# On VectorE, the second set of masks of the scan ahead of the turn of the next tile's raw blocks

## The chip, the cores and the metric

The kernel runs on one core of one Trainium2 chip. The metric is the device time of one execution in microseconds, lower is better. Five engines work side by side, each on its own queue of instructions: TensorE (PE, matrix products and transposes), VectorE (DVE), ScalarE (ACT), GpSimd (POOL) and SyncE (SP), which here only issues transfers. They meet at semaphores that the program names itself.

## The reference

One inference step of a one-layer backbone over 17 tiles of 128 tokens: 16 tiles of latent tokens and one of context. Only the time-mixing part matters here, a recurrence in two directions with 8 heads and a 64 x 64 state:

```python
def step(S, inp):
    r_t, w_t, k_t, v_t, kk_t, kka_t = inp
    sa = jnp.einsum('bdhvk,bdhk->bdhv', S, kk_t)
    S = (S * w_t[..., None, :] - sa[..., :, None] * kka_t[..., None, :]
         + v_t[..., :, None] * k_t[..., None, :])
    return S, jnp.einsum('bdhvk,bdhk->bdhv', S, r_t)

s_final, ys = lax.scan(step, s0.astype(f32), xs)
```

Before it the tokens are normed, modulated and projected; after it three branches are gated, merged and projected, and a mixture of 16 experts and a final norm follow.

## The kernel before

The stages run one after the other: tokens (`stage_tokens`), the recurrence (`stage_scan`), the merge, the routing, the experts, and the last norm. `stage_scan` takes most of the time between 950 and 1900 us of the profiled span, and only it is touched.

**How the scan works.** It walks over 17 tiles, in both directions at once (`d` is the direction, `g` one of two groups of four heads). Within a tile the recurrence is written in block form, so that it turns into products of 128-token blocks and the inverse of a triangular 128 x 128 matrix for each head. Products of scaled rows give four sets of blocks: the raw blocks `Ar` (Q by B), from which the inverse is made, and the mixed blocks `ArbT`, `AqkT` and `ArkT`. VectorE multiplies each mixed set by a triangular mask on its way out of PSUM: four instructions for each set (two directions by two groups), at line L1253. These are the masks in the title.

**The inverse goes round through DRAM, a tile ahead.** In step `q` the raw blocks of tile `q + 1` are made (TensorE `raw`, copied out by ScalarE at L1063). Those of direction 1 must be turned first: `turn_raw` on VectorE (two transposes into `AT`, tile name b_at, semaphore `at_ok`). ScalarE then writes their diagonal blocks to DRAM (`backward_out`, L927), as SyncE does for direction 0 (`forward_out`). When all eight small writes have landed (`a_st`), SyncE reads them back in another layout (`diagonal_in`, b_ta, L947), GpSimd inverts them (`invert`, L918 and L921), SyncE writes the result out (`inverse_out`, s_t, L955) and, in the step after, places it in `TZ` (`inverse_in`, b_tz, L967), which VectorE turns and TensorE uses.

**SyncE's queue is in order.** In one step it issues: `inverse_out(q)`, `forward_out(q + 1)`, `inverse_in(q)`, `diagonal_in(q + 1)`, then the four loads of the input rows of tile `q + 2` (`front`, in `load_front`, L133; semaphore `f_in[d]`, 2.5 MB), then the outputs of the last tile and the next values. All that stands behind `diagonal_in` waits with it.

**Who waits for the input rows.** On ScalarE `own_decay(q + 2, d)` (an exponential, L1029) waits for `f_in[d]` and stands ahead of the copies `u6` (L1131) and `tl` (L1135) that TensorE's product `w6` of the present tile needs. On TensorE `cumulate(q + 2, d)` (two products of 128 x 512 for each direction in the records) waits for `f_in[d]` and stands right ahead of `w6`. Both exist in steps 0 to 14.

**TensorE's order in a step** is: transposes, raw products of tile `q + 1`, the mixed products (`arb`, `aqk`, `ark`), then XX (state and `AqkT` by values, reads `aqk_ok`), the inverse's steps u5, w5, u6, the transposes `tl`, `cumulate`, w6, the product u, the new state n, and the outputs y. The masks of `AqkT` are what XX waits for. The last step (tile 16) has no next tile, so no `turn_raw` and no `cumulate`.

`over_tiles` writes steps 0, 1, 14, 15 and 16 out and runs steps 2 to 13 in a loop of two steps each. The order of every engine is that of the program text; nothing is scheduled behind it.

Of the kernel before, what the change touches and what calls it, by code (L numbers as in the profile page):

```python
# [87 lines left out]
def after(e, sem, t, per=1):  # L88

    e.wait_ge(sem, t * per + per)  # L90


def freed(e, sem, t, per=1):

    if not (isinstance(t, int) and t == 0):
        e.wait_ge(sem, t * per)
# [702 lines left out]
def stage_scan(nc, io, scr, K):  # L799
# [3 lines left out]
    with ExitStack() as ctx:  # L803
# [3 lines left out]
        def each(name, shape):  # L807
            return [sb(f"b_{name}{d}", shape) for d in range(2)]
# [15 lines left out]
        def by_four(ap):  # L824
            return ap.rearrange("p (j n) -> p j n", j=4)
# [14 lines left out]
        ArbT, AqkT, ArkT = (each(n, [P, H, P]) for n in ("arbT", "aqkT", "arkT"))  # L840
# [52 lines left out]
        def heads(g):  # L893
            return slice(4 * g, 4 * g + 4)

        def over_group(c):
            return const[:, c, :].unsqueeze(1).broadcast_to([P, 4, P])

        def flat(ap):
            return ap.rearrange("p a n -> p (a n)")  # L900

        def bank(d, i):
            return ps[:, 4 * d + i, :]

        def by_head(ap):
            return ap.rearrange("p (h n) -> p h n", h=H)
# [22 lines left out]
        with nc.Block() as block:  # L929
# [249 lines left out]
            def _(dve):  # L1179
# [3 lines left out]
                def turn(out, src, g):  # L1183

                    return v_.transpose(flat(out[:, heads(g), :]), flat(src[:, heads(g), :]))

                def before_token(t, d):

                    after(dve, f_in[d], t, 32)
                    after(dve, x_ok[d], t)  # L1190
                    v_.tensor_tensor(EX[d][:, :], F[d][:, FKK, :], EX[d][:, :], ALU.mult).then_inc(kx_ok[d], 1)

                def scaled_q(t, d):
                    after(dve, e_ok[d], t)
                    after(dve, kx_ok[d], t)
                    freed(dve, qT_ps[d], t)
                    v_.tensor_tensor(Qt[d][:, :], EX[d][:, :], EI[d][:, :], ALU.mult).then_inc(q_ok[d], 1)

                def scaled_b(t, b, d):

                    if not (isinstance(t, int) and t < 2):
                        after(dve, n_ps[d], t - 2)
                    after(dve, e_ok[d], t)
                    v_.scalar_tensor_tensor(Bt[d][b][:, :], F[d][:, FKA, :], -1.0, EN[d][:, :], ALU.mult, ALU.mult)\
                        .then_inc(b_ok[d], 1)

                def turn_raw(t, b):
                    freed(dve, a_st, t, 128)
                    for d, g in (PAIRS[0][1], PAIRS[1][0]):
                        after(dve, ar_ok[1][g], t)  # L1210
                        turn(AT, Ar[1][b], g).then_inc(at_ok, 1)

                def scaled_state(own, d, factor):
                    return v_.tensor_tensor(Shd[d][own, :, own], SN[d][own, :, :],
                                            factor[own].broadcast_to([64, 4, N]), ALU.mult)
# [21 lines left out]
                def step(q, b, n, left):  # L1237
                    if left > 1:
                        for d in range(2):
                            after(dve, pm_ok[d], q + 1)  # L1240
                            after(dve, shd_ok[d], q)
                            v_.tensor_tensor(fac[d][:, :].unsqueeze(2), PM[d][b][:, :, 1:2], PM[d][1 - b][:, :, 0:1], ALU.mult)\
                                .then_inc(fac_ok[d], 1)
                    for d in range(2):
                        after(dve, rT_ps[d], q)
                        v_.tensor_copy(flat(RT[d][:, :, :]), bank(d, 0)).then_inc(rT_ok[d], 1)
                    for out, p_ps, p_ok, at, masks in ((ArbT, arb_ps, arb_ok, (0, 2), (UPI, LOWI)),
                                                       (AqkT, aqk_ps, aqk_ok, (1, 3), (UP, LOW)),
                                                       (ArkT, ark_ps, ark_ok, (0, 2), (UPI, LOWI))):
                        for r, pair in enumerate(PAIRS):  # L1250
                            for d, g in pair:
                                after(dve, p_ps[d][g], q)
                                v_.tensor_tensor(out[d][:, heads(g), :], by_four(bank(d, at[r])), over_group(masks[d]), ALU.mult)\  # L1253
                                    .then_inc(p_ok[d][g], 1)
                        if out is ArbT and left > 0:
                            turn_raw(q + 1, 1 - b)
                    for d in range(2):
                        after(dve, tz_in[d], q, 64)
                        for g in range(2):
                            turn((TIT[0], TI[1])[d], TZ[d], g).then_inc(turn_ok[d][g], 1)  # L1260
                    for d, g in GROUPS:
                        after(dve, w5_ps[d][g], q)
                        after(dve, turn_ok[d][g], q)
                        v_.tensor_tensor(TIT[d][:, heads(g), :], (TIT[0], TZ[1])[d][:, heads(g), :],
                                         by_four(bank(d, 2 * g + 1)), ALU.add).then_inc(tr5_ok[d][g], 1)
                    if left > 1:
                        for d in range(2):
                            before_token(q + 2, d)
                    for d in range(2):
                        after(dve, w6_ps[d], q)  # L1270
                        v_.tensor_copy(TIT[d][LO[d], :, HI[d]], by_head(bank(d, 1))[LO[d]]).then_inc(t6_ok[d], 1)
                    if left > 1:
                        for d in range(2):
                            scaled_q(q + 2, d)
                    for d in range(2):

                        after(dve, n_ps[d], q)
                        after(dve, shd_ok[d], q)
                        new = by_four(bank(d, 2))
                        for u in range(2):  # L1280
                            own = slice(64 * u, 64 * u + 64)
                            ins = v_.tensor_tensor(SN[d][own, :, :], Shd[d][own, :, own], new[own, :, own], ALU.add)
                        ins.then_inc(sn_ok[d], 1)
                    if left > 1:
                        for d in range(2):
                            scaled_b(q + 2, b, d)
                    for d in range(2):
                        after(dve, y_ps[d], q)
                        freed(dve, y_st[d], q, 16)
                        v_.tensor_copy(Yo[d][:, :], bank(d, 1)).then_inc(y_ok[d], 1)  # L1290
                        after(dve, sn_ok[d], q)
                        if left > 1:
                            after(dve, fac_ok[d], q)
                            for u in range(2):
                                ins = scaled_state(slice(64 * u, 64 * u + 64), d, fac[d][:, :].unsqueeze(2))
                            ins.then_inc(shd_ok[d], 1)
                        elif left == 1:
                            v_.memset(Shd[d][:, :, :], 0.0).then_inc(shd_ok[d], 1)
                        else:
                            v_.tensor_tensor(SN[d][:, :, :], SN[d][:, :, :], PM[d][b][:, :, 1:2].broadcast_to([P, 4, N]),  # L1300
                                             ALU.mult).then_inc(s_ok[d], 1)

                over_tiles(dve, step)

            @block.tensor
# [1202 lines left out]
```

## Time and profile before

| | us |
|---|---|
| median of 3 runs | 3972.12 (3970.88 to 3974.76) |
| profiled execution | 3966.32 |
| its span | 3964.5 |
| TensorE busy in it | 3638.9 (92%) |
| VectorE, ScalarE, GpSimd busy | 1398.0, 785.9, 1046.8 |
| mean granted TensorE clock | 0.949 of full |

The profile is of one execution. A row of the timeline gives start, duration, engine, line and operation with the program's tile names, count and, in square brackets, the idle time of the engine before it and what ended that. The timeline merges neighbouring instructions of one kind. The granted clock is 1.00 at 2.4 GHz and 0.50 at 1.2 GHz.

### The profile page before, as it was taken

The numbers are of one execution on the slowest core, as the hardware profiler recorded it, in microseconds if no ns is written. First come the engines' busy times: TensorE is split into PE (matmuls) and PEld (weight loads), VectorE is DVE, ScalarE is ACT, GpSimd is POOL, SyncE is SP. The second block draws the span as 40 slices with busy tenths as digits, with TensorE's granted clock in tenths as the row PEclk, the third lists the DMA queues.
The fourth block names the chain that finished last, engine by engine and source line by source line (L and its number), as shares of the span: only waits on it lengthen the run. The fifth ranks groups of instructions, "written<-read, shape, count | busy, mean of one in ns | idle before, by whom it ended". The sixth has DMA issues, their size and how long they took to land. (4 is left out here: it accounts for less than half of the span.)

```text
span 3964.5 us, 64158 instructions
## 1 busy us (share of the span) xinstructions
PE 3638.9 (92%) x24967; PEld 2884.9 (73%) x24968; DVE 1398.0 (35%) x2878; ACT 785.9 (20%) x1467; POOL 1046.8 (26%) x1506
## 2 busy tenths in 40 slices
PE   8999999996899999999799999999999949999960
PEld 4676666674798999999789989989989934444420
DVE  2444444443645444444121222222222242222227
ACT  1222222222333333332011111111111101111113
POOL 0333333332455555554011011011011000000013
PEclk9999999997899999999899999999999969999985
DMA  8323222324332333331711011011011144765236
GB/s 291 107 101 104 92 92 88 105 96 147 97 102 67 90 100 102 102 102 36 270 45 65 35 41 65 35 41 65 35 44 61 43 165 165 259 226 187 90 107 216
DMA packets 296969, 424.33 MB, mean 107 GB/s; under 512 B 122415, under 2 KB 205997, under 8 KB 296749
## 3 DMA queue, kind: packets, MB, share of 16 engines
q1 hardware_dynamic: 259244, 349.55, 26.4%
q0 software_dynamic: 11952, 43.52, 3.3%
q10 hardware_dynamic: 25552, 27.93, 2.0%
q8 instruction: 187, 3.06, 0.3%
q14 instruction: 34, 0.27, 0.0%
HBM read 287.99 MB, written 132.94 MB: 106 GB/s over the span
## 5 line engine op out<-in xcount | busy, mean ns | idle before, releaser
L1808 PE MATMUL c_ps<-c_hT,big 128*128 128x128 f32 x6528 | 752.7, 276 | 25.1 <-DMA big<-in_w_in 25.1
L1808 PEld LDWEIGHTS c_ps<-c_hT,big 128*128 128x128 f32 x6528 | 743.9, 193 | 33.0 <-issue 29.3
L695 PE MATMUL a_ps<-front,a_hT 128*128 128x512 f32 (+1 forms) x1088 | 416.1, 540 | 3.5 <-DVE a_mix L597 3.5
L2231 PE MATMUL e_ps<-big,e_xT 128*128 x784 | 347.5, 596 | 2.3 <-DVE e_xT L2193 2.3
L695 PEld LDWEIGHTS a_ps<-front,a_hT 128*128 128x128 f32 x1088 | 204.0, 190 | 199.5 <-issue 187.0
L689 PE MATMUL a_ps<-a_hT,front 128*128 128x128 f32 x2992 | 344.7, 277 | 2.3 <-ACT a_hT L360 2.3
L689 PEld LDWEIGHTS a_ps<-a_hT,front 128*128 128x128 f32 x2992 | 341.4, 193 | 6.2 <-issue 2.9
L2231 PEld LDWEIGHTS e_ps<-big,e_xT 128*128 128x128 f32 x784 | 149.4, 191 | 191.7 <-issue 191.7
L918 POOL TENSOR_TENSOR b_tmp<-b_tt,b_ta 128x126 f32<-128x126 f32 (+22 forms) x496 | 191.2, 386 | 246.4 <-DMA b_ta<-s_a 208.8
L1808 PE MATMUL c_ps<-c_wo,c_mT 128*128 128x512 f32 x544 | 236.3, 592 | 0.0
L1773 DVE TENSOR_TENSOR c_gs<-c_gs,c_ps 128x384 f32<-128x384 f32 x136 | 75.4, 554 | 445.0 <-PE c_ps L1808 434.7
L1308 PE MATMUL b_ps<-front 64*128 64x128 f32 (+3 forms) x1972 | 199.7, 290 | 34.4 <-PEq L125 19.7
L921 POOL TENSOR_TENSOR b_tt<-b_tt,b_tmp 128x126 f32<-128x126 f32 (+22 forms) x496 | 201.4, 406 | 38.9
L1308 PEld LDWEIGHTS b_ps<-front 64*128 64x128 f32 (+1 forms) x1972 | 172.0, 193 | 48.0 <-issue 44.1
L1672 ACT ACTIVATE c_gs<-c_ps 128x384 f32<-128x384 f32 x136 | 66.5, 489 | 674.9 <-DVE c_mT L1776 603.9
L1698 POOL TENSOR_TENSOR c_yb<-c_yb,c_lnx 128x512 f32<-128x512 f32 x17 | 21.5, 1265 | 662.1 <-DVE c_yb L1751 662.1
L1808 PEld LDWEIGHTS c_ps<-c_wo,c_mT 128*128 128x128 f32 x544 | 102.1, 190 | 122.0 <-issue 122.0
L2150 POOL DMA_INDIRECT e_x<-s_h,src x49 | 46.1, 941 | 511.9 <-PE e_ps L2237 465.5
L2231 PE MATMUL e_ps<-big,e_aT 128*128 x392 | 177.8, 596 | 1.6 <-DVE e_aT L2201 1.6
L1808 PE MATMUL c_ps<-c_cs,c_wp 128*128 128x128 f32 x1088 | 158.4, 276 | 0.0
L1308 PE MATMUL b_ps<-b_shd,front 128*128 128x128 f32 x544 | 131.3, 326 | 28.0 <-issue 28.0
L1808 PE MATMUL c_ps<-c_yT,c_wp 128*128 128x128 f32 x1088 | 143.7, 275 | 0.0
(317 smaller groups left out, 5093.7 us busy)
## 6 DMA issues: line engine op xcount, KB each, us to landing
big<-in_exp_w SPq DMA_DIRECT2D x48, 1024.0 KB, 10.2
s_D<-a_shared SPq DMA_DIRECT2D x34, 768.0 KB, 6.0
front<-s_D SPq DMA_DIRECT2D x34, 768.0 KB, 7.3
s_yr<-e_yo ACTq DMA_DIRECT2D x49, 512.0 KB, 3.0
front<-s_A SPq DMA_DIRECT2D x34, 512.0 KB, 5.9
a_aw<-in_ada_w SPq DMA_DIRECT2D x32, 512.0 KB, 6.6
s_A<-a_shared SPq DMA_DIRECT2D x17, 768.0 KB, 3.4
big<-in_w_in SPq DMA_DIRECT2D x12, 1024.0 KB, 12.2
```

What stands on the lines that cost most here:

```text
L689: ins = nc.tensor.matmul(ps[:, bank, j * P:(j + 1) * P], win[:, k, c:c + P], hT[b][:, k, :], start=k == 0, stop=k == KD - 1)
L695: ins = nc.tensor.matmul(ps[:, bank, 0:width], hT[b][:, k, :], win[:, k, c:c + width], start=k == 0, stop=k == KD - 1)
L918: g_.tensor_tensor(part, TT[:, i0:HR, k:k + 1].broadcast_to([P, m, k]), TA[:, k:k + 1, 0:k].broadcast_to([P, m, k]), ALU.mult).then_inc(tm ...
L921: g_.tensor_tensor(TT[:, i0:HR, 0:k], TT[:, i0:HR, 0:k], part, ALU.add).then_inc(ts_ok, 1)
L1308: return nc.tensor.matmul(out, lhsT, rhs, start=start, stop=stop)
L1672: a(Gs[j % 2][:, :], ps[:, GB[j % 3], 0:3 * P], ACT.Sigmoid).then_inc(s["G_ok"], 1)
L1698: g.tensor_tensor(yb[:, :], yb[:, :], lnx[:, :], ALU.mult).then_inc(s["yw_ok"], 1)
L1773: v.tensor_tensor(Ms[j % 2][:, :], Gs[j % 2][:, :], ps[:, PB[j % 2], 0:3 * P], ALU.mult)\
L1808: return nc.tensor.matmul(out, lhsT, rhs, start=start, stop=stop)
L2150: pool.indirect_dma_start(X[b % S][:, :], None, scr["h2"].rearrange("t p n -> (t p) n"), bass.IndirectOffsetOnAxis(K["src"][:, b:b + 1], 0 ...
L2231: return nc.tensor.matmul(out, lhsT, rhs, start=start, stop=stop)
```

## The change

In the loop of step `q` over the three mixed sets on VectorE, `turn_raw(q + 1)` is called after the masks of `AqkT` instead of after those of `ArbT`:

```diff
@@ -1252,7 +1252,7 @@
                                 after(dve, p_ps[d][g], q)
                                 v_.tensor_tensor(out[d][:, heads(g), :], by_four(bank(d, at[r])), over_group(masks[d]), ALU.mult)\
                                     .then_inc(p_ok[d][g], 1)
-                        if out is ArbT and left > 0:
+                        if out is AqkT and left > 0:
                             turn_raw(q + 1, 1 - b)
                     for d in range(2):
                         after(dve, tz_in[d], q, 64)
```

It takes effect in steps 0 to 15. No instruction is added or removed, and the other engines' instructions stand as before.

VectorE before, in an odd step of the loop: b_arbT, b_aqkT and b_arkT are the three masked sets, b_at the turned raw blocks of the next tile, b_tz the inverse, b_tiT and b_ti its turned forms.

```order
L1253 TENSOR_TENSOR b_arbT0<-b_ps,front 128x512
L1253 TENSOR_TENSOR b_arbT1<-b_ps,front 128x512 x2
L1253 TENSOR_TENSOR b_arbT0<-b_ps,front 128x512
L1185 STREAM_TRANSPOSE b_at<-b_ar10 128x512 x2
L1253 TENSOR_TENSOR b_aqkT0<-b_ps,front 128x512
L1253 TENSOR_TENSOR b_aqkT1<-b_ps,front 128x512 x2
L1253 TENSOR_TENSOR b_aqkT0<-b_ps,front 128x512
L1253 TENSOR_TENSOR b_arkT0<-b_ps,front 128x512
```

The same place now:

```order
L1253 TENSOR_TENSOR b_arbT0<-b_ps,front 128x512
L1253 TENSOR_TENSOR b_arbT1<-b_ps,front 128x512 x2
L1253 TENSOR_TENSOR b_arbT0<-b_ps,front 128x512
L1253 TENSOR_TENSOR b_aqkT0<-b_ps,front 128x512
L1253 TENSOR_TENSOR b_aqkT1<-b_ps,front 128x512 x2
L1253 TENSOR_TENSOR b_aqkT0<-b_ps,front 128x512
L1185 STREAM_TRANSPOSE b_at<-b_ar10 128x512 x2
L1253 TENSOR_TENSOR b_arkT0<-b_ps,front 128x512
```

The four masks of `AqkT` moved up past two transposes, and the transposes down past four masks; the masks of `ArkT` stay where they were.

ScalarE, in an even step, is the same in both kernels; it is shown since it reads b_at and the input rows. The write of b_at (L927) stands here, and the exponentials of the input rows (L1029) stand ahead of the copies for TensorE (L1131).

```order
L1063 ACTIVATE b_ar<-b_ps 128x512 x4
L90 ISA x2
L927 DMA s_a<-b_at 32x8x32 x4
L96 REGISTER_ALU
L1085 ACTIVATE b_tt<-front 128x512
L1119 ACTIVATE front<-b_ps 128x512 x2
L1122 ACTIVATE b_u<-b_ps 128x512 x4
L1074 ACTIVATE b_al<-b_ar 32x8x32 x4
L90 ISA
L1029 ACTIVATE front<-front 128x512 x2
L1131 ACTIVATE b_u<-b_ps 64x8x64 x2
```

Nothing moved on ScalarE; what it waits for at L927 now comes later on VectorE.

## Rows read from the trace of the kernel before

**Rows 1.** The page: engines, and 40 slices of the span with TensorE's granted clock.
```profile
PE 3638.9 (92%) x24967; PEld 2884.9 (73%) x24968; DVE 1398.0 (35%) x2878; ACT 785.9 (20%) x1467; POOL 1046.8 (26%) x1506
...
PEclk9999999997899999999899999999999969999985
```

**Rows 2.** Timeline of VectorE in step 8: start, us, engine, line, tiles, count.
```profile
1445.53 2.48 DVE L1253 TENSOR_TENSOR b_arbT<-b_ps,front 128x512 f32<-128x512 f32 x4 [3.77 <-PE b_ps L1308]
1447.94 1.29 DVE L1185 STREAM_TRANSPOSE b_at<-b_ar 128x512 f32<-128x512 f32 x2
1449.15 2.44 DVE L1253 TENSOR_TENSOR b_aqkT<-b_ps,front 128x512 f32<-128x512 f32 x4
1451.52 2.46 DVE L1253 TENSOR_TENSOR b_arkT<-b_ps,front 128x512 f32<-128x512 f32 x4
```

**Rows 3.** Timeline of TensorE in step 8: aqk and ark, XX, cumulate, w6, u.
```profile
1446.23 3.77 PE L1308 MATMUL b_ps<-front 64*128 64x128 f32 x64
...
1451.80 0.48 PE L1308 MATMUL b_ps<-b_shd,front 128*128 128x128 f32 x2 [1.80 <-issue]
...
1467.43 1.98 PE L1308 MATMUL b_ps<-front 128*128 128x512 f32 x4
1469.34 1.90 PE L1308 MATMUL b_ps<-b_u,b_ti 64*64 64x64 f32 x32
1471.26 3.79 PE L1308 MATMUL b_ps<-front,b_tiT 128*128 128x64 f32 x32
```

**Rows 4.** Waits of TensorE and ScalarE, scan steps 0 to 16: total us, times, longest.
```profile
PE b_ps L1308 <- issue: 28.0, 17, 1.8
PE b_ps L1329 <- issue: 9.8, 5, 2.2
...
ACT front L1029 <- DMA front<-s_D: 14.2, 9, 2.9
```

**Rows 5.** Timeline of the last step (tile 16) on TensorE: XX, w6, u.
```profile
1866.09 0.46 PE L1308 MATMUL b_ps<-b_shd,front 128*128 128x128 f32 x2 [0.51 <-issue]
...
1882.22 1.87 PE L1308 MATMUL b_ps<-b_u,b_ti 64*64 64x64 f32 x32 [0.46 <-ACT b_ti L1135]
1884.11 6.21 PE L1308 MATMUL b_ps<-front,b_tiT 128*128 128x64 f32 x32
```

**Rows 6.** Timeline of SyncE's issues in step 8: diagonal_in, last load of the input rows.
```profile
1452.91 1.13 SPq L947 DMA_DIRECT2D b_ta<-s_a  x2
...
1456.17 0.58 SPq L133 DMA_DIRECT2D front<-s_D  x1
```

**Rows 7.** Timeline of ScalarE in step 8: own_decay of both directions, u6, tl.
```profile
1463.40 0.63 ACT L1029 ACTIVATE front<-front 128x512 f32<-128x512 f32 x1
1465.94 0.63 ACT L1029 ACTIVATE front<-front 128x512 f32<-128x512 f32 x1 [1.91 <-DMA front<-s_D]
1466.48 1.19 ACT L1131 ACTIVATE b_u<-b_ps 64x512 f32<-64x512 f32 x2
1467.69 1.21 ACT L1135 ACTIVATE b_ti<-b_ps 64x512 f32<-64x512 f32 x2
```

**Rows 8.** Timeline of step 9, a step with the lower clock: masks, XX, w6.
```profile
1495.80 2.49 DVE L1253 TENSOR_TENSOR b_arbT<-b_ps,front 128x512 f32<-128x512 f32 x4 [3.38 <-PE b_ps L1308]
...
1501.97 0.46 PE L1308 MATMUL b_ps<-b_shd,front 128*128 128x128 f32 x2 [1.70 <-issue]
...
1524.36 1.90 PE L1308 MATMUL b_ps<-b_u,b_ti 64*64 64x64 f32 x32
```

**Rows 9.** Windows: length, busy PE, PEld, DVE, ACT, POOL, granted clock, DMA share, GB/s.
```profile
1503.00:1513.00 10.00, 10.00 (x49) 10.00 (x48) 3.65 (x7) 1.19 (x2) 4.15 (x14) 0.50 0.87 271
...
1438.00:1441.00 3.00, 3.00 (x16) 3.00 (x15) 0.69 (x1) 1.68 (x3) 0.68 (x1) 0.50 0.00 0
...
1885.00:1895.00 10.00, 10.00 (x49) 10.00 (x49) 0.84 (x2) 1.19 (x2) 0.00 (x0) 0.51 0.00 0
```

**Rows 10.** Timeline of GpSimd: its shortest idle between an inversion and the next work.
```profile
1757.36 1.28 POOL L1161 TENSOR_TENSOR front<-front 128x512 f32<-128x512 f32 x1 [3.43 <-PE b_ps L1329]
```

## The prediction

> **What bounds the kernel now.** I read the page first: TensorE is busy 92% of the span, and its granted clock dips most in the tenth and eleventh of the 40 slices, where the scan begins; the scan goes on to slice 19, and its later falls are too short for this view [rows 1]. So time is to be won or lost in the scan where TensorE stands idle or runs at the lower of its two levels (1.2 instead of 2.4 GHz). Then the waits of the scan: TensorE waited 17 times before XX, 28.0 us in all, and 5 times before the first transposes of a step, 9.8 us in all; those five are at the turn of the loop, and the change doesn't touch them [rows 4]. ScalarE waited 9 times, 14.2 us in all, for the input rows of the tile after next [rows 4]. Then the timelines of one step for each engine. I take step 8 as the pattern and count from its first `ArbT` mask, A = 1445.53 [rows 2].
>
> **The wait before XX.** TensorE ends the ark products at 1446.23 + 3.77 = 1450.0 and starts XX at 1451.80 [rows 3]; the last `AqkT` mask ends at 1449.15 + 2.44 = 1451.59 [rows 2]. The record calls the wait "issue", but its end follows the mask by 0.21 us, so the mask is what ends it. Fifteen of the steps 0 to 15 show 1.70 to 1.81 us there and step 0 shows 1.41; step 16, which has no turn of raw blocks, shows 0.51 [rows 5].
>
> **Part one, the masks come earlier.** The two transposes take 1449.15 - 1447.94 = 1.21 us from start to start [rows 2]. Without them ahead, the masks of `AqkT` run from 1447.94 to 1450.38. Their products are ready: half of the aqk and ark products, thus all of aqk, is done by about 1448.1 [rows 3]. XX starts at about 1450.6, 1.2 us earlier, and 0.6 us of idle remain, close to the 0.51 of step 16. By itself that is 16 x 1.2 = 19 us.
>
> **Part two, the clock in XX.** In 6 of the 17 steps (3, 5, 7, 9, 11, 14) the clock fell to 0.50 just behind this wait and stayed there for 10.2 us (the first window of [rows 9]). The price: w6 starts 1524.36 - 1495.80 = 28.56 us after A in step 9 [rows 8] and 1469.34 - 1445.53 = 23.81 in step 8 [rows 2, 3], so 4.75 us in each of the six. With a pause of 0.6 us instead of 1.75 I expect these falls to be gone; step 16 kept its clock through XX behind 0.51 us.
>
> **Part three, the turn comes later, and what stands behind it.** The transposes end 2.37 us later: four masks from start to start, 1451.52 - 1449.15 [rows 2]. Their followers are ScalarE's writes, then SyncE's `diagonal_in`, which starts 1452.91 - 1449.23 = 3.68 us after the transposes' end [rows 2, 6] and waits for those writes (in step 9 it stood idle 0.55 us before it). So it moves by the whole 2.37 us, and with it all that is queued behind it: the four loads of input rows, the outputs of the last tile and the next values. GpSimd's inversion starts 2.37 us later too; its shortest idle before its next work is 3.43 us [rows 10], so that costs nothing. The outputs and values have most of a step. The input rows have no slack: ScalarE already waits for them in the nine steps that kept their clock (0, 1, 2, 4, 6, 8, 10, 12, 13), 1.58 us in the mean [rows 4], 1.91 in step 8 [rows 7].
>
> In step 8 the rows of direction 1 landed at 1465.94; now 1468.31. Behind that wait stand the `u6` and `tl` copies: from the wait's end to the start of the first `tl` copy 1.75 us, the copy 0.61, and the signal some 0.1 (as in step 16, where TensorE waited for this copy), in sum 2.5 [rows 7]. So w6 starts at about 1470.8 instead of 1469.34 [rows 3], 1.46 us later, although XX was 1.2 earlier. With the mean wait in place of step 8's (0.33 less) it is 1.13 later. In A's count: landing 22.43, w6 at 24.93, against 22.6 if nothing but XX counted.
>
> **The sum with the clock left alone.** Nine steps that had their clock: 9 x +1.13 = +10.2. Six that lost it in XX: 24.93 - 28.56 = -3.63 each, -21.8. Step 15 has no input rows to wait for: -1.2. Together -12.8 us: two thirds of the gain of part one go into the new wait.
>
> **Part four, the clock at the new wait.** This term decides the sign. The new idle is not spread. `cumulate` would start 1.2 us earlier than now, and half of it takes 0.98 [rows 3]. In A's count TensorE thus ends its first half at 1467.43 - 1.2 + 0.98 - 1445.53 = 21.67, stands still to 22.43 (the rows of direction 1), works 0.98, and stands still again from 23.4 to 24.93 (ScalarE's copies): 2.3 us of idle with 1.0 us of work between, and behind them w6, products of 64 x 64 on 64 rows [rows 3]. What do rows show of such stretches? Pauses of 1.70 to 1.81 us before XX were followed by a fall in 6 of 15; pauses of 1.83 to 2.20 us at the loop's turn in 4 of 4 (the second window of [rows 9] lies in one), and one of 1.58 us there in none. Nearest of all is step 16: a pause of only 0.46 us right before w6, and the clock fell from 1885.1 to 1895.3 [rows 5, 9]; a like pause of 0.47 us in step 15 left it. The new stretch is emptier than each of these and lies in the same kind of products. I take it that the clock falls there in all fifteen steps 0 to 14.
>
> The Trainium skill ("TensorE: Matmul & The Clock Gate", section "Why this matters for your kernels") advises against pauses longer than any here, and one who goes by it would count on the clock holding. The falls behind 1.7 us and 0.46 us speak against reading it so. Its result is the first rival below.
>
> The price of a fall, by step 16: 10.2 us at half clock, thus 5.1 us. Bounds: one short fall of 3.4 us costs 1.7 (the loop's turn [rows 9]); the most is all of w6 and u, 1.90 + 3.79, at half clock and a piece of the products behind [rows 3], some 6.8 us. I take 5.1, the same place in the same stage: 15 x 5.1 = +76.5. With -12.8 the sum is +64 us, and the profiled 3966.3 would become 4030; against the median of 3972.1 it is 4036. Ends: 15 x 6.8 - 12.8 = +89; with half of the falls 7.5 x 5.1 - 12.8 = +25. A few us more either way come from the turn of the loop, where the four falls of 1.7 us may come or go.
>
> **The rivals.**
>
> *Faster: the clock holds at w6.* The new wait is two short pauses and not one, the `cumulate` products between them are the longest of the stage, and steps 0 to 14 had no fall at this place before. Then the first sum stands: -13 us, 3959. It decides at about one fall in six: 12.8 / 5.1 = 2.5 falls of 15 make the change neutral. Chance 0.12. A milder form, 3 to 7 falls, gives +3 to +25 us; chance 0.09.
>
> *The input rows are not later.* If `diagonal_in` did not follow the turn, or the transfers made up the time since less collides with them, w6 would start at 22.6: 9 x -1.2, 6 x -5.95, -1.2, in sum -48 us, 3924. Against it: SyncE's issues follow each other in order, and the transfers moved together. A partial form (half the lateness made up) has smaller pauses, perhaps without falls. Chance 0.04.
>
> *XX keeps its falls.* If the clock falls in XX behind 0.6 us as it did behind 1.75, the slow steps gain 1.2 each and need no new wait: +10.2 - 7.2 - 1.2 = +2 us, with the nine others open to falls at w6: up to +48. Chance 0.05. That the change does nothing is not to be had: the order on VectorE is as written and both ends of it are waited for.
>
> **How the numbers follow.** Forecast, falls at w6 in eight or more of the fifteen steps: 0.70, 3997 to 4065, likeliest 4036. The range 3982 to 4068 holds this case whole, the upper part of the milder one, and part of the last: 0.80. About 0.2% (8 us) is what a measurement of this kernel can tell from no change. Faster by more: 0.12 + 0.04 = 0.16. Within it: 0.05 of the milder form, 0.02 of the last: 0.07. Slower: 0.77.
>
> **What would show it.** XX should start 5.1 us after A behind 0.6 us of idle, in all steps, and no fall in XX. `diagonal_in` should start 9.8 us after A (7.4 before). ScalarE's wait before L1029 for the input rows should be there in 15 steps, with 4 us or so in place of 1.6, since it also comes to it 1.2 us earlier. TensorE should show new waits before the second half of `cumulate` (for the transfer) and before w6 (for ScalarE's b_ti), and the granted clock 0.50 for some 10 us from w6 on, in nearly each step. The steps would last about 56 us where good ones lasted 50.3. If w6 starts at 22.6 after A, part three is wrong; if it starts at 24.9 and the clock stays at 1.00, part four is wrong and the kernel is faster.

## The result

The change made the kernel slower. Median of seven runs 4005.46 us (3985.55 to 4012.17) against 3972.12 us for the kernel before (seven runs, 3970.08 to 3974.76): 33 us, a ratio of 1.0068 with a 95% interval of 1.0042 to 1.0093. The profiled execution took 3985.55 us (span 3983.8), which is at the low end of these runs and 19.2 us above the profiled execution of before. The sign was forecast; of the size, 4036 us stood in the text. The seven executions differ by their clock: the mean granted clock was 0.946 in the profiled one, 0.945 in the two near 3990 us, and 0.940 to 0.941 in the four at 4005 us and above.

All start times below that are given "after the first mask" count from the start of the first `ArbT` mask of the step. The counterpart of [rows 2] is the timeline of VectorE in step 8 of the changed kernel (start, us, engine, line, tiles, count). The masks of `AqkT` follow those of `ArbT` at once, and the turn (b_at) starts 4.80 us after the first mask instead of 2.41:

```profile
1444.90 2.48 DVE L1253 TENSOR_TENSOR b_arbT<-b_ps,front 128x512 f32<-128x512 f32 x4 [3.38 <-PE b_ps L1308]
1447.31 2.47 DVE L1253 TENSOR_TENSOR b_aqkT<-b_ps,front 128x512 f32<-128x512 f32 x4
1449.70 1.29 DVE L1185 STREAM_TRANSPOSE b_at<-b_ar 128x512 f32<-128x512 f32 x2
```

The counterpart of [rows 3], TensorE in the same step: XX (b_shd), both halves of `cumulate`, w6 (b_u,b_ti) and u (b_tiT):

```profile
1449.98 0.48 PE L1308 MATMUL b_ps<-b_shd,front 128*128 128x128 f32 x2 [0.61 <-issue]
...
1465.61 1.12 PE L1308 MATMUL b_ps<-front 128*128 128x512 f32 x2
1467.60 1.12 PE L1308 MATMUL b_ps<-front 128*128 128x512 f32 x2 [0.87 <-DMA front<-s_D]
1470.07 1.87 PE L1308 MATMUL b_ps<-b_u,b_ti 64*64 64x64 f32 x32 [1.34 <-ACT b_ti L1135]
1471.95 3.79 PE L1308 MATMUL b_ps<-front,b_tiT 128*128 128x64 f32 x32
```

XX's pause is 0.61 us instead of 1.80. In its place stand two new pauses further on, 0.87 us for the input rows and 1.34 us for ScalarE's copies. w6 starts 1470.07 - 1444.90 = 25.17 us after the first mask, where it was 23.81. SyncE's issues and ScalarE's waits of the step answer to [rows 6] and [rows 7]:

```profile
1454.18 1.13 SPq L947 DMA_DIRECT2D b_ta<-s_a  x2
...
1463.54 0.63 ACT L1029 ACTIVATE front<-front 128x512 f32<-128x512 f32 x1 [1.98 <-DMA front<-s_D]
1467.58 0.63 ACT L1029 ACTIVATE front<-front 128x512 f32<-128x512 f32 x1 [3.42 <-DMA front<-s_D]
1468.12 1.19 ACT L1131 ACTIVATE b_u<-b_ps 64x512 f32<-64x512 f32 x2
1469.33 1.21 ACT L1135 ACTIVATE b_ti<-b_ps 64x512 f32<-64x512 f32 x2
```

And the waits of the whole scan, against [rows 4] (total us, times, longest):

```profile
ACT front L1029 <- DMA front<-s_D: 74.4, 30, 3.4
...
PE b_ps L1308 <- ACT b_ti L1135: 20.6, 16, 1.3
...
PE b_ps L1329 <- issue: 8.8, 5, 1.9
PE b_ps L1308 <- issue: 8.5, 16, 0.6
...
PE b_ps L1308 <- DMA front<-s_D: 6.6, 11, 1.1
```

TensorE's wait before XX fell from 28.0 to 8.5 us. Against it stand 27.2 us of waits that the late rows brought, 20.6 us for ScalarE's copies and 6.6 us for the rows themselves. ScalarE's own wait for them grew from 14.2 to 74.4 us.

In this execution the clock fell behind w6 in 7 of the 15 steps 0 to 14 (steps 6, 7, 9, 10, 11, 13, 14), five times for 10.2 us and twice for 13.7, and never in XX. Step 9 is one of them. Behind XX its only pause was the 1.34 us before w6, and u took 7.06 us instead of 3.79:

```profile
1520.61 1.87 PE L1308 MATMUL b_ps<-b_u,b_ti 64*64 64x64 f32 x32 [1.34 <-ACT b_ti L1135]
1522.50 7.06 PE L1308 MATMUL b_ps<-front,b_tiT 128*128 128x64 f32 x32
```

The window that answers to [rows 9] (length, busy times of PE, PEld, DVE, ACT, POOL, granted clock, DMA share, GB/s):

```profile
1523.00:1533.00 10.00, 10.00 (x49) 10.00 (x49) 1.73 (x3) 1.37 (x3) 8.59 (x19) 0.51 0.00 0
```

Step 8 had both pauses, 2.2 us in sum, and kept its clock. So the length of the pause doesn't settle in which step the clock falls.

### The profile page after: what moved, and what is told of

The parts are those of the page before. It is cut to its first block and busy times, and to the rows that moved or that the text cites. A ratio compares the mean times of both kernels' runs of the same rounds, so it can differ in the third digit from the quotient of the medians.

```text
span 3983.8 us, 64158 instructions
## 1 busy us (share of the span) xinstructions
PE 3648.8 (92%) x24967; PEld 2889.5 (73%) x24968; DVE 1400.0 (35%) x2878; ACT 783.6 (20%) x1467; POOL 1046.5 (26%) x1506
## 3 DMA queue, kind: packets, MB, share of 16 engines
q1 hardware_dynamic: 259244, 349.55, 26.3%
## 5 line engine op out<-in xcount | busy, mean ns | idle before, releaser
L1308 PE MATMUL b_ps<-front 64*128 64x128 f32 (+3 forms) x1972 | 215.7, 299 | 40.7 <-DMA front<-s_D 20.4
L1308 PEld LDWEIGHTS b_ps<-front 64*128 64x128 f32 (+1 forms) x1972 | 183.3, 202 | 59.4 <-issue 36.4
L452 DVE SCALAR_TENSOR_TENSOR a_part<-a_aw,a_sil,a_part 128x128 f32<-128x128 f32 x448 | 142.6, 391 | 0.0
## 6 DMA issues: line engine op xcount, KB each, us to landing
big<-in_exp_w SPq DMA_DIRECT2D x48, 1024.0 KB, 10.2
```

What stands on the lines that cost most here:

```text
L452: ins = nc.vector.scalar_tensor_tensor(own, aw[:, k, :], sil[:, 8 * v + k:8 * v + k + 1], own, ALU.mult, ALU.add)
L1308: return nc.tensor.matmul(out, lhsT, rhs, start=start, stop=stop)
```

## The experiments

All are timed against the kernel before on the same chip. Beside these later runs the kernel before spread more than it had at first (3938 to 3992 us in one series of 25), so ratios are given and not times.

### The changed kernel again

> The changed kernel once more, unaltered, for a second profile: its seven times so far lie between 3985.6 and 4012.2 us, far wider than the 4.7 us of the kernel before. If the number of clock falls behind the pause before w6 is what varies, this profile shows the same waits (XX 5.0 us after the first ArbT mask, w6 24.1 to 25.4) and another number of falls, and its time differs from 3985.6 by about 5.1 us for each fall of 10.2 us more or less. If it is the transfers that vary, the landing of the input rows differs from the 22.2 us of the first profile.

Six runs lay between 3986.66 and 4019.89 us, ratio 1.0091 (1.0059 to 1.0122). The profile (3986.66 us) shows the waits of the first: w6 at 23.4 to 25.8 us, again seven falls behind w6, in other steps (5, 7, 9, 10, 11, 12, 14). A third series:

> The changed kernel unaltered, for its ratio beside turn_first_again on the same chip, and a third profile. Rows at 22 us, w6 at 24 to 25.5, six to nine falls behind w6 in steps 0 to 14, ratio 1.006 to 1.010.

Nine runs from 3983.76 to 4017.08, ratio 1.0090 (1.0059 to 1.0121). This time nine falls stood behind w6 (seven of them 13.7 us long) and four at the turn of the loop; the profiled execution took 3999.98 us. From 1020 to 1900 us of the span the clock was at half for 99.0 us in the first profile and 129.7 us in this one. Half of the difference is 15.4 us, and the two executions differ by 14.4. What varies between these executions is thus mostly how much of the scan runs at 1.2 GHz.

### The late turn without the early masks

```diff
                        for r, pair in enumerate(PAIRS):
                            for d, g in pair:
...
+                            if out is AqkT and r == 0 and left > 0:
+                                turn_raw(q + 1, 1 - b)
-                        if out is ArbT and left > 0:
-                            turn_raw(q + 1, 1 - b)
```

> The turn between the first two and the last two masks of AqkT. XX waits for the fourth of these masks, so it starts no earlier than in the kernel before (6.2 us, pause 1.7 to 1.8 us), while the turn ends 1.2 us later. It is the price of the changed order without its gain. Theory: falls in XX as before in some steps; in the others the rows land near 21 us instead of 20, w6 up to 1 us late, one or two falls there: 10 to 25 us slower, ratio 1.002 to 1.006. Rival (the early masks cost something themselves, say by XX colliding with other work): ratio 1.000.

Ratio 0.9993 (0.9967 to 1.0019): no difference that can be measured. XX kept its pause, 1.70 to 1.83 us in steps 1 to 15, and fell in five steps; in the ten others the rows landed between 20.7 and 22.7 us, w6 started between 23.7 and 25.2, and the clock fell behind w6 once. The direction inside the steps is as expected, the total is below the expected range and is the number that the rival had named. The rival's reason, that the early masks cost something themselves, doesn't fit the pair with the rows moved, further down, where early masks gain. A turn that is half as late costs next to nothing by itself; in five steps the fallen clock of XX hides it, and the pauses that it leaves before w6 are shorter than the changed kernel's (none in four steps, 0.49 to 0.84 us in five, 1.33 in one).

### The late rows alone

```diff
-                    if left > 1:
-                        front(q + 2, two)
                     for d in range(2):
...
                             load_v(one[d], d, 1 - b)
+                    if left > 1:
+                        front(q + 2, two)
```

> The kernel before, VectorE's order untouched; on SyncE the loads of the input rows stand behind the outputs of the last tile and the next values (1 MB) instead of ahead of them, so they land 2.5 to 3 us later. It is the lateness of part three alone. Theory: the nine steps that kept their clock show a pause before w6 like the changed kernel's, w6 at 25 to 25.5 us after the first mask (23.8 before), falls there in about half of them; the XX falls of the other steps stay. 9 x 1.5 + 4 or 5 x 5.1 = 34 to 39 us slower, ratio 1.009. Rival (lateness without early masks costs only the wait): 14 us, ratio 1.0035.

Ratio 1.0049 (1.0030 to 1.0068), between the expected 1.009 and the rival's 1.0035. Ten steps reached w6 with their clock. There the rows landed between 21.4 and 23.8 us and w6 started between 24.2 and 26.3, as in the changed kernel. The clock fell behind w6 in two of them, fewer than the expected half: both are among the five with a pause of 1.24 to 1.34 us before w6, and none among the four with 0.40 to 0.69. Step 1 is one:

```profile
1087.62 1.98 PE L1308 MATMUL b_ps<-front 128*128 128x512 f32 x4
1090.85 2.00 PE L1308 MATMUL b_ps<-b_u,b_ti 64*64 64x64 f32 x32 [1.24 <-ACT b_ti L1135]
```

VectorE's order is that of the kernel before here. The pause before w6 thus comes with late rows alone, and some falls with it.

### Filling the pauses with products that nobody reads

```diff
-                        for d in range(2):
-                            cumulate(q + 2, d)
+                        cumulate(q + 2, 0)
+                        mm(bank(1, 3), const[:, CUMI[0], :], F[0][:, FSG, :])
+                        cumulate(q + 2, 1)
+                        for i in range(2):
+                            mm(bank(0, 2)[HI[0], :], const[:, CUMI[0], 0:64], F[0][:, FSG, :])
```

> The changed kernel with three added products of 512 columns on TensorE in steps 0 to 14, whose results nobody reads: one between the two halves of cumulate, two (into the free half of a bank) behind it, ahead of w6. They fill about 1.5 us of the 1.8 us in which TensorE stands idle there. w6 waits for ScalarE as before and starts at most 0.3 us later. Theory (the pause causes the falls): falls at w6 nearly gone, the sum with the clock left alone holds, about 13 us under the kernel before, ratio 0.997, between 0.995 and 1.000. Rival (the small products of w6 and u cause the falls): as many falls as in the changed kernel, ratio 1.007 or more.

Ratio 0.9981 (0.9962 to 0.9999), beside 1.0091 for the changed kernel on the same chip, and the ten runs lay within 12.5 us of each other. It is the decisive run. Step 8, `cumulate` with the added products, then w6 and u:

```profile
1459.42 4.85 PE L1308 MATMUL b_ps<-front 128*128 128x512 f32 x10
1464.19 1.90 PE L1308 MATMUL b_ps<-b_u,b_ti 64*64 64x64 f32 x32
1466.11 3.79 PE L1308 MATMUL b_ps<-front,b_tiT 128*128 128x64 f32 x32
```

TensorE does some 2.9 us more work in each of 15 steps and starts w6 later than the changed kernel does, 25.57 us after the first mask in the mean against 24.69, and the kernel is nevertheless faster than the changed one by 1.1% (median 3962.06 against 4004.58 us). The rows are as late as in the changed kernel (ScalarE waits 76.2 us for them). But no step from 0 to 14 lost its clock, neither in XX nor at w6. The granted clock of the scan, this kernel first, then the changed one and the one before (columns as above):

```profile
1030.00:1840.00 810.00, 788.97 (x7999) 727.02 (x7998) 393.68 (x666) 277.53 (x537) 463.62 (x1033) 0.99 0.33 94
```

```profile
1030.00:1860.00 830.00, 785.18 (x7875) 748.15 (x7874) 391.75 (x664) 277.07 (x536) 454.73 (x1020) 0.94 0.33 92
```

```profile
1030.00:1840.00 810.00, 773.10 (x7860) 741.81 (x7860) 388.26 (x662) 280.62 (x537) 453.52 (x1016) 0.95 0.34 94
```

So the loss of the changed kernel is the clock, and the clock comes back when this stretch is filled. One thing stays open: at the turn of the loop TensorE still paused five times, for 1.59 to 2.23 us, and lost its clock in none, where the kernel before had lost it four times in five. The added products may thus do more than close the pause before w6; the two weren't separated. My expectation had a step wrong: I took an added product to last 0.49 us, and it lasts 0.98 us, since the records count two for each of width 512. So the added work, and not a wait, sets the start of w6.

### The read of the diagonal blocks on ScalarE's queue

```diff
+                def diagonal_in(t):
+                    after(act, a_st, t, 128)
+                    for half in range(2):
+                        act.dma_start(flat(TA[64 * half:64 * half + 64, :, :]), scr["a32"]).then_inc(ta_in, 16)
...
                         identity(q + 1)
+                        diagonal_in(q + 1)
```

SyncE no longer issues it in the steps, and waits for the last placing of the inverse before it writes the next.

> The changed kernel, but the read of the diagonal blocks (diagonal_in) of steps 0 to 15 is issued by ScalarE behind its own writes, not by SyncE. Nothing then stands between inverse_in and the four loads of input rows in SyncE's queue: they start about 7.1 us after the first ArbT mask instead of 10.7. Theory (the late input rows make the pause, the pause the falls): they land near 20 us, the pause of TensorE before w6 goes, w6 starts at 22.6, no fall at w6 and none in XX: 9 x 1.2 + 6 x 5.95 + 1.2 = 48 us under the kernel before, ratio 0.988. Rival (the falls belong to the products of this stretch, once XX starts early, not to the wait): w6 at 22.6 but falls stay, ratio 1.000 or more. Rival (transfers share the same engines, so an earlier issue lands no earlier): as the changed kernel, 1.007.

Ratio 0.9977 (0.9953 to 1.0001), half-way and by another road than expected. The rows were early only in some steps. In six steps ScalarE issued its read 9.6 to 10.2 us after the first mask, while the row loads were still on their way, and the rows of direction 1 landed at 21.4 to 22.6 us all the same; where the read went out at 11.4 us or later they landed by 18.4 to 20.6 as far as a wait shows it. Step 7 is of the first kind:

```profile
1398.82 1.13 ACTq L1087 DMA_DIRECT2D b_ta<-s_a  x2
...
1410.47 0.63 ACT L1030 ACTIVATE front<-front 128x512 f32<-128x512 f32 x1 [4.55 <-DMA front<-s_D]
```

In this step the transfer engines were busy throughout, but moved 286 GB/s in four microseconds in which the read came in (14 to 18 us after the first mask), and 378 GB/s ahead of them (columns as above):

```profile
1398.74:1401.74 3.00, 3.00 (x30) 3.00 (x29) 1.31 (x2) 1.74 (x4) 0.00 (x0) 1.00 0.98 378
1402.74:1406.74 4.00, 4.00 (x39) 3.86 (x38) 2.31 (x4) 2.88 (x6) 0.00 (x0) 1.00 1.06 286
```

Five falls stood behind w6, all in steps with rows at 21.7 us or later. The third theory, that an earlier issue need not land earlier, holds in these six steps. In steps of the second kind TensorE waited up to 0.9 us for ScalarE's U copies, which stood behind the issue. In steps 0 and 14, where the read went out as late as 15.5 and 18.7 us, it waited 3.3 and 7.3 us for them, and in step 14 the clock fell in this wait. That cost is of this way of issuing the read, and part of why the expected 0.988 was missed.

### The work on the rows moved behind w6, with and without the change

```diff
                     for d in range(2):
                         lo = LO[d]
...
                         ins.then_inc(w6_ps[d], 1)
+                    if left > 1:
+                        for d in range(2):
+                            cumulate(q + 2, d)
```

with `cumulate` taken out ahead of w6, and in the same way `own_decay` put behind the `tl` copies on ScalarE and `before_token` behind the `t6` copies on VectorE.

> The changed kernel, with what waits for the input rows moved behind what TensorE needs for this tile: on ScalarE own_decay behind the u6 and tl copies, on TensorE cumulate behind w6, on VectorE before_token behind the t6 copies. The rows still land 22.2 us after the first ArbT mask, but w6 no longer waits for them. Theory: w6 at 21.1 as in the last step, cumulate at 23 behind it, the u product at 25 where good steps of the kernel before had it at 25.7; no fall in XX, few at w6 (the pause there is 0.46 us, as in the last two steps, which lost their clock in three of four cases, but 2 us of full-width products now follow at once). 48 us under the kernel before if no fall is left, 20 us if about half of the steps lose their clock: ratio 0.988 to 0.995. Rival (early masks are worth nothing by themselves): ratio 1.000 or more.

Ratio 0.9914 (0.9883 to 0.9944), within the expected span. w6 starts 21.1 to 21.2 us after the first mask (21.8 in step 0), and four of the steps 0 to 14 lost their clock there.

> The same move of the work on input rows, in the kernel before, with VectorE's turn where it was. In the steps that keep their clock the rows cost TensorE nothing there (w6 is bound by XX), so only their order changes: the u product no later and at most 0.3 us earlier. XX keeps its pause of 1.7 to 1.8 us and its falls in some six steps. Ratio 1.000, between 0.997 and 1.002. If it is as fast as rows_after, the move and not the earlier masks is what gains.

Ratio 1.0086 (1.0056 to 1.0117), where no difference was expected. Where XX kept its clock, w6 starts at 22.3 to 22.8 us, earlier than in the kernel before, and yet the clock fell behind it in nine of the steps 0 to 14, besides five times in XX (once in step 15). Step 4, from `tl` on:

```profile
1258.54 1.02 PE L1457 MATMUL b_ps<-ident,b_tiT 64*128 64x64 f32 x16
1260.02 2.70 PE L1306 MATMUL b_ps<-b_u,b_ti 64*64 64x64 f32 x32 [0.47 <-ACT b_ti L1132]
1262.65 3.78 PE L1306 MATMUL b_ps<-front 128*128 128x512 f32 x4
```

A pause of 0.47 us was followed by a fall here, in the picture of [rows 5]: the wide `cumulate` products no longer stand ahead of w6, and 64 x 64 work lies on both sides of the pause. That this order is the reason is not shown. The three kernels with it (this pair and the last one below) had 16 falls in 45 such steps: nine in this kernel, four in the other of the pair, three in the last. With `cumulate` ahead, pauses of 0.40 to 0.84 us before w6 stood in ten steps of other kernels here, and one was followed by a fall. In the kernel before, `cumulate` filled just this place and covered ScalarE's copies. Between the two kernels of this pair only VectorE's order differs: 0.9914 against 1.0086. Early masks, with the late turn that goes with them, are worth some 1.7% where TensorE doesn't wait for the rows.

### The turn ahead of all masks

```diff
+                    if left > 0:
+                        turn_raw(q + 1, 1 - b)
                     for out, p_ps, p_ok, at, masks in ((ArbT, arb_ps, arb_ok, (0, 2), (UPI, LOWI)),
...
-                        if out is ArbT and left > 0:
-                            turn_raw(q + 1, 1 - b)
```

> The kernel before, with the turn of the raw blocks ahead of the ArbT masks. The first transpose falls into VectorE's idle time (3.4 to 3.8 us before the first mask), the second puts the masks back by some 0.6 us. Theory: XX's pause falls from 1.75 to 1.1 us, the diagonal blocks are read no later than before (SyncE's own queue sets 7.1 us), the rows land near 19.8, w6 at 23.2 and no pause before it, fewer falls in XX: 15 x 0.6 = 9 us and up to 6 x 4.75 = 28 us of falls, ratio 0.991 to 0.998. Rival (lateness of the turn is not what made the changed kernel slow): no better than the changed kernel.

> The turn ahead of the ArbT masks once more, beside the changed kernel on the same chip, since only four times stood behind its ratio of 0.988. XX's pause 1.2 to 1.3 us, rows at 19 to 20 us, w6 at 22.5, at most one or two falls outside the turn of the loop. Ratio to the kernel before 0.986 to 0.991. If the first result was a lucky placing of the falls, 0.995.

Ratio 0.9884 (0.9823 to 0.9945) with four runs, then 0.9894 (0.9860 to 0.9928) with six, beside 1.0090 for the changed kernel on the same chip. The first is better than the 0.991 that was expected at best. VectorE in step 8 of the second:

```profile
1422.00 1.30 DVE L1185 STREAM_TRANSPOSE b_at<-b_ar 128x512 f32<-128x512 f32 x2 [2.87 <-ACT b_ar L1063]
1423.23 2.45 DVE L1255 TENSOR_TENSOR b_arbT<-b_ps,front 128x512 f32<-128x512 f32 x4
1425.60 2.47 DVE L1255 TENSOR_TENSOR b_aqkT<-b_ps,front 128x512 f32<-128x512 f32 x4
```

The turn starts as soon as ScalarE has copied the raw blocks, in time in which VectorE stood idle, and the masks follow without a gap. TensorE:

```profile
1428.27 0.48 PE L1308 MATMUL b_ps<-b_shd,front 128*128 128x128 f32 x2 [1.28 <-issue]
...
1443.89 1.98 PE L1308 MATMUL b_ps<-front 128*128 128x512 f32 x4
1445.80 1.90 PE L1308 MATMUL b_ps<-b_u,b_ti 64*64 64x64 f32 x32
```

XX's pause is 1.28 us, no fall stands in XX in either profile, and w6 follows `cumulate` without a pause in 26 of the 30 steps (0 to 14 in both). One of them lost its clock behind w6, step 13 of the first, where the rows landed at 21.2 us and TensorE paused for 1.18; step 11 of the second, with rows at 21.2 and a pause of 1.21, kept it.

> Turn of the raw blocks ahead of the ArbT masks and the work on input rows behind w6, both together. XX's pause 1.1 us, rows near 19.8 and nobody waits for them. Theory: 10 to 35 us under the kernel before, ratio 0.991 to 0.998, not as good as rows_after if that keeps its clock, since XX starts 0.6 us later in each of 16 steps.

Ratio 0.9938 (0.9908 to 0.9968): as expected, and not better than the turn ahead alone. Three steps lost their clock behind w6, each behind a bare pause of 0.47 us as in the pair above, and one in XX.

## Why the prediction was right in direction and wrong in size

**What was read first.** The page's lowest slices of the granted clock are the fortieth (5) and the thirty-third (6), both outside the scan; the tenth and eleventh (7 and 8) are only among the lowest. No term of the sum rests on this.

**Part one held.** XX starts 5.0 to 5.1 us after the first mask behind 0.51 to 0.61 us, in steps 1 to 16, as forecast.

**Part two held.** No fall in XX in three profiles of the changed kernel, against six in the one of before; the pair with the rows moved says the same from the other side, with five falls in XX where the masks are late and none where they are early. Over steps 1 to 15 of all profiles, pauses of 1.70 to 1.83 us before XX were followed by a fall in 21 of 60 cases, pauses of 1.18 to 1.32 in 1 of 45, and pauses of 0.51 to 0.64 in none of 90.

**Part three held, slightly too dear.** In step 8 `diagonal_in` moved from 7.4 to 9.3 us after the first mask, 1.9 us and not 2.37. The prediction took it to start when ScalarE's writes had landed. In step 8 of the kernel before, it followed the end of `inverse_in` (L967) in SyncE's queue by 0.3 us; the queue had held it, and some of the turn's lateness fell into that slack:

```profile
1448.81 3.78 SPq L967 DMA_DIRECT2D b_tz<-s_t  x8
1452.91 1.13 SPq L947 DMA_DIRECT2D b_ta<-s_a  x2
```

In the changed kernel `inverse_in` ended 2.1 us ahead of it, and the writes are what it waited for (over the scan, SyncE's wait for them at this place grew from 2.3 to 23.9 us). The rows landed at 22.2 us in the mean (forecast 22.4) and w6 started at 24.69 (forecast 24.93). ScalarE waited in both directions, 74 us in place of the 60 (15 x 4) that I had named. GpSimd was not held up: behind an inversion it still stood idle for at least 2.28 us before its next work.

**Part four named the right place and mis-sized it; this is the step that failed.** I let the clock fall in all fifteen steps. It fell in seven, seven and nine. The price of a fall was within its bounds: half of its length is 5.1 us for those of 10.2 us and 6.8 for those of 13.7. Read from the steps it is a little less: from w6 to the next step's first mask there are 26.4 us with the clock kept, 31.2 to 31.3 behind a fall of 10.2 us and 32.7 to 32.8 behind one of 13.7 (all three profiles, where no turn of the loop lies between; 32.1 once, where the fall began ahead of w6), so 4.8 and 6.3. With the terms of this profile the sum is: nine steps 9 x (24.69 - 23.81) = +7.9; six steps 6 x (24.69 - 28.56) = -23.2; step 15 -1.2; falls 5 x 5.1 + 2 x 6.8 = +39.1; the turn of the loop, two falls of 1.7 us less and 9.8 - 8.8 = 1.0 us less idle, -4.4; a fall in step 15 of 13.7 us where there was one in step 16 of 10.2, +1.7. Together +19.9; the two profiled executions differ by 19.2, and with the falls at 4.8 and 6.3 us the same sum is about +17, so an agreement within 1 us is partly luck. The forecast had +76.5 where +39 stood. Two of the three profiled executions, with seven falls, are the milder form that had been given a chance of 0.09; the line "with half of the falls +25" was nearer than the likeliest value. The medians differ by 33 us and not by 19: the lower clock of the slower executions goes with more time at 1.2 GHz, as in the third profile. The falls in them weren't counted.

The error was to argue from the emptiness of the new stretch to a fall in every step. The trace of before already had the warning: pauses of like length before XX were followed by a fall in 6 of 15. A share like that, 15 x 6/15 = 6, and a few more for the emptier stretch, was what rows bore out. The share itself is now measured (23 of 45). What picks the steps is not shown by any run here and stays open.

The advice of the Trainium skill ("TensorE: Matmul & The Clock Gate", section "Why this matters for your kernels"), which warns of pauses longer than any of these before XX and w6, would have given the faster rival. The measurement decides against it: pauses of 1.34 us and of 0.47 us were followed by falls, and added products that nobody reads took the falls away.

**The rivals.** The faster one (clock holds, -13 us) was wrong for this kernel, but its sum is borne out by the filled kernel: that one keeps its clock and lies 0.2% under the kernel before, with 0.9 us more to w6 in each step. The row lateness was not made up, and XX kept no falls.

**The range** held the median of 4005 us, but the likeliest value stood 31 us above it.

## What to carry to other kernels

Before an operation is moved back past another on an in-order engine, follow its result to the next in-order queue and read what stands behind it there. Here two transposes, 1.2 us together, that stood 2.4 us later held back 2.5 MB of loads that had no slack. Look first for idle time of the engine ahead of both: the turn fitted into VectorE's idle time, of which 2.9 us are left ahead of it, and gave 1.1% where the change lost 0.7 to 0.9%. And where TensorE pauses among small products, price the pause with the clock that follows it, by the share of such pauses that were followed by a fall and not by the worst.

## What the runs showed of the hardware

- Products that nobody reads, 2.9 us of them in each of 15 steps, made the kernel 1.1% faster than the same kernel without them: the granted clock of the scan went from 0.94 to 0.99.
- At one place (before XX) the share of pauses that were followed by a fall went with their length: 21 of 60 at 1.70 to 1.83 us, 1 of 45 at 1.18 to 1.32, none of 90 at 0.51 to 0.64.
- At another place a pause of 0.47 us was enough: before w6, among 64 x 64 products on both sides, it was followed by a fall in 16 of 45 steps. With 128 x 512 products just ahead, one of ten pauses of 0.40 to 0.84 us was. The difference between the places is shown, the reason isn't.
- The same program took from 3985.55 to 4012.17 us. Two of its profiles with nearly the same waits differ by 14.4 us, and half of the difference of their time at 1.2 GHz is 15.4 us.
- A read of 0.5 MB on a second queue, issued right behind 2.5 MB of loads, delayed them: they landed 21.7 us after the first mask instead of 18.4 (steps 7 and 8 of the kernel with the read on ScalarE). Up to 0.9 us of this may come from their own later issue. While the read came in, the engines moved 286 GB/s instead of 378.
